# The in-chunk products A on all four quarters of TensorE's array, in two banks, with ScalarE carrying half of them across partitions

## The reference

```python
def step(S, inp):
    r_t, w_t, k_t, v_t, a_t, b_t = inp
    Sa = jnp.einsum("bhvk,bhk->bhv", S, a_t)
    S = S * w_t[:, :, None, :] + Sa[..., None] * b_t[:, :, None, :] + v_t[..., None] * k_t[:, :, None, :]
    y = jnp.einsum("bhvk,bhk->bhv", S, r_t)
    return S, y
...
h = rms_norm(x, g_mix[i])
proj = h @ w_in[i]
y_a = rwkv7_time_mix(proj[..., :RW_COLS], ...)
y_b = dilated_mixture_attention(proj[..., RW_COLS:], slopes)
gate_a, gate_b = jnp.split(jax.nn.sigmoid(h @ w_gate[i] + b_gate[i]), 2, axis=-1)
merged = gate_a * (y_a @ w_branch_a[i]) + gate_b * (y_b @ w_branch_b[i])
x = x + merged @ w_out[i]
x = x + conv_glu_ffn(rms_norm(x, g_ffn[i]), w_up[i], conv_w[i], conv_b[i], w_down[i])
ple_gate = jax.nn.sigmoid(rms_norm(x, g_ple[i]) @ w_ple_gate[i])
x = x + ple_gate * (p[i] @ w_ple[i])
```

## Time and profile before

| what | value |
|---|---|
| median of three runs | 955.06 us |
| profiled execution | 956.54 us |
| its span (first to last instruction) | 954.7 us |
| TensorE busy | 933.7 us, 98% of the span |
| VectorE, ScalarE, GpSimd busy | 43%, 45%, 40% |
| mean granted TensorE clock | 0.997 |

### The profile page before, as it was taken

One profiled execution on the slowest core, in us unless ns is written; L12 is line 12 of the kernel. 1 busy time (PEld: TensorE's weight loads), 2 busy tenths in 40 slices (PEclk: granted clock), 3 DMA queues, 4 the chain that ended last, 5 costly groups with the idle time before them and its releaser, 6 DMA issues.

```text
span 954.7 us, 15908 instructions
## 1 busy us (share of the span) xinstructions
PE 933.7 (98%) x6783; PEld 769.9 (81%) x6783; DVE 409.4 (43%) x645; ACT 428.6 (45%) x683; POOL 384.9 (40%) x180
## 2 busy tenths in 40 slices
PE   6999999999999999999999999999999999999996
PEld 5887888897778778788788888888888888888885
DVE  4223798308565548559244434434344300100435
ACT  6355553235554644623445344443444411412647
POOL 2453444442223526246423444444444444445350
PEclk9999999999999999999999999999999999999998
DMA  7432433332121000226412333333333332323132
GB/s 250 129 92 64 110 88 90 88 90 67 45 59 33 27 25 25 68 71 216 134 44 67 89 106 93 92 107 89 103 96 90 110 110 99 100 89 119 63 105 89
DMA packets 115163, 86.59 MB, mean 91 GB/s; under 512 B 2852, under 2 KB 100022, under 8 KB 115094
## 3 DMA queue, kind: packets, MB, share of 16 engines
q1 hardware_dynamic: 114904, 85.50, 30.3%
q10 hardware_dynamic: 190, 0.08, 0.0%
HBM read 83.47 MB, written 2.10 MB: 90 GB/s over the span
## 4 chain that ended last, share of the span: by engine, by line
PE 95%; ACT 2%; DVE 1%; POOL 1%; DMA 1%; issue 0%; SPq 0%; DVEq 0%
PE bank L544 19%; PE bank L545 18%; PE bank L546 18%; PE bank L606 9%; PE bank L607 9%; PE bank L608 9%; PE bank L863 2%; PE bank L734 1%; PE bank L771 1%; PE bank L819 1%; PE bank L748 1%; POOL w_lo L524 1%; DMA xs<-in_x_dram 1%; PE bank L860 1%; PE bank L904 0%; PE bank L830 0%
## 5 line engine op out<-in xcount | busy, mean ns | idle before, releaser
L524 POOL TENSOR_TENSOR w_lo<-raw,w_hi 128x1024 fp32r<-128x1024 f32 x137 | 330.5, 2412 | 490.4 <-ACT w_hi L1144 490.3
L1144 ACT ACTIVATE w_hi<-raw 128x1024 fp32r<-128x1024 f32 x137 | 145.4, 1061 | 339.6 <-issue 201.2
L544 PE MATMUL bank<-hT_hi,w_hi 128*128 128x512 f32 (+1 forms) x720 | 282.1, 392 | 1.2 <-POOL w_lo L524 1.0
L546 PE MATMUL bank<-hT_hi,w_lo 128*128 128x512 f32 (+1 forms) x720 | 277.0, 385 | 0.0
L545 PE MATMUL bank<-hT_lo,w_hi 128*128 128x512 f32 (+1 forms) x720 | 277.0, 385 | 0.0
L544 PEld LDWEIGHTS bank<-hT_hi,w_hi 128*128 128x128 f32 x720 | 135.2, 188 | 29.3 <-issue 1.7
L546 PEld LDWEIGHTS bank<-hT_hi,w_lo 128*128 128x128 f32 x720 | 135.3, 188 | 27.1
L545 PEld LDWEIGHTS bank<-hT_lo,w_hi 128*128 128x128 f32 x720 | 135.4, 188 | 25.1
L2052 DVE SCALAR_TENSOR_TENSOR cbuf<-bank,params,cbuf 128x511 f32<-128x511 f32 x48 | 36.0, 750 | 132.9 <-ACT cbuf L1542 132.9
L606 PE MATMUL bank<-w_hi,g_hi 128*128 128x512 f32 x184 | 71.7, 390 | 0.0
L608 PE MATMUL bank<-w_hi,g_lo 128*128 128x512 f32 x184 | 71.6, 389 | 0.0
(11 more groups left out here) (318 smaller groups left out, 1350.4 us busy)
## 6 DMA issues: line engine op xcount, KB each, us to landing
raw<-in_w_up_dram SPq DMA_DIRECT2D x48, 512.0 KB, 3.8
raw<-in_w_in_dram SPq DMA_DIRECT2D x33, 512.0 KB, 4.0
raw<-in_w_down_dram SPq DMA_DIRECT2D x24, 512.0 KB, 3.8
raw<-in_w_gate_dram SPq DMA_DIRECT2D x16, 512.0 KB, 4.0
raw<-in_w_out_dram SPq DMA_DIRECT2D x8, 512.0 KB, 4.1
raw<-in_w_ple_gate_dram SPq DMA_DIRECT2D x8, 512.0 KB, 4.2
xs<-in_x_dram SPq DMA_DIRECT2D x4, 512.0 KB, 5.3
raw<-in_w_branch_a_dram SPq DMA_DIRECT2D x4, 512.0 KB, 3.4
```

Of the source, the lines that this page charges most:

```text
L524: nc.gpsimd.tensor_tensor(low(n)[:, :], raw[:, n % RAW_SLOTS, :], high(n)[:, :].bitcast(F32), ALU.subtract).then_inc(*step("pool", ("lo", n)))
L544: nc.tensor.matmul(o, wh, ah, start=first, stop=False)
L546: return nc.tensor.matmul(o, wl, ah, start=False, stop=last)
L1144: nc.scalar.activation(high(u)[:, :], raw[:, u % RAW_SLOTS, :], ACT.Copy) \
```

## The change

`product_a` now takes two banks per group. The products of one chunk are no longer kept to the two quarters on the diagonal: a product of head q (rows of half q) and chunk s is written to the columns of half s. The bank is the first where s = q and the second where s is not q. ScalarE reads them with three copies: the first bank with all 128 partitions, and the two halves of the second bank each into the other half of the partitions, so that `Am` again holds head q in half q. In `Am`, `XT` and `Xs` chunk s of head q now lies in slot s xor q of its group, so `solved_u` picks `Xs` by `c % 2 ^ q`.

```diff
-                o = begin("A", g)
-                head_products(o, lambda s, p, q: KK[half(q), p, chunk_cols(2 * g + s)],
-                              lambda s, p, q: Kb[half(q), p, 2 * g + s, 0, :]).then_inc(*step("pe", ("A", g)))
+                o = [begin("A", g, slot) for slot in range(2)]
+                for p in range(NPAIR):
+                    for s, q in ((0, 0), (1, 1), (1, 0), (0, 1)):
+                        mm = nc.tensor.matmul(o[s ^ q][half(s), p * CH:(p + 1) * CH], KK[half(q), p, chunk_cols(2 * g + s)],
+                                              Kb[half(q), p, 2 * g + s, 0, :], start=True, stop=True)
+                mm.then_inc(*step("pe", ("A", g)))
...
-                        mm = nc.tensor.matmul(o[q][half(0), p * CH:(p + 1) * CH], Xs[half(q), c // 2, c % 2, p, :],
+                        mm = nc.tensor.matmul(o[q][half(0), p * CH:(p + 1) * CH], Xs[half(q), c // 2, c % 2 ^ q, p, :],
...
-                nc.scalar.activation(flat(Am[:, g, :, :, :]), psum(("A", g))[:, :], ACT.Copy) \
-                    .then_inc(*frees("act", ("A", g), ("Am", g)))
+                nc.scalar.activation(Am[:, g, 0, :, :].rearrange("p h t -> p (h t)"), psum(("A", g, 0))[:, 0:256], ACT.Copy) \
+                    .then_inc(*frees("act", ("A", g, 0)))
+                nc.scalar.activation(Am[half(0), g, 1, :, :].rearrange("p h t -> p (h t)"), psum(("A", g, 1))[half(1), 0:256],
+                                     ACT.Copy).then_inc(*step("act"))
+                nc.scalar.activation(Am[half(1), g, 1, :, :].rearrange("p h t -> p (h t)"), psum(("A", g, 1))[half(0), 0:256],
+                                     ACT.Copy).then_inc(*frees("act", ("A", g, 1), ("Am", g)))
```

More of the change, by code:

```diff
@@ L786, in _ @@
             token_units([("v1", s) for s in range(2)], [("vt1", m) for m in range(NT)], hT_hi, hT_lo, 4, 256)
[L792 to L800, removed]
             def chunk_cols(c):
```

## The result

| | before | after |
|---|---|---|
| median | 954.79 us (22 runs, 953.18 to 955.8) | 963.25 us (22 runs, 952.96 to 967.68) |
| profiled execution | 956.54 us | 963.06 us |
| its span | 954.7 us | 961.2 us |
| mean granted TensorE clock | 0.997 | 0.987 |

A forecast was written before the change was run, and what follows sets the result against it. TensorE, busy 98% of the span, was taken as the bound. Products -1.9 us, waiting for `Xs` +1.9, later start +0.1 gave +0.1 us: median 955.2 us, range 953.2 to 957.0.

The forecast's parts named there:

- TensorE's products, 0.49 us a group: Products A on TensorE: four groups take 1.96 us, 0.49 each instead of 0.93, so 1.9 us less work.
- ScalarE's copies, 1.215 us a group: Copies to `Am` on ScalarE: three per group, 1.215 us from group to group, 4.86 us in all instead of 2.4.
- `Am` as late as the identity: Group 0: `Am` ready 0.15 us later than before, arriving together with GpSimd's identity, so VectorE's masked copy starts no earlier.
- the possible 0.25 us: Partial gain possible if VectorE's masked copy takes 0.80 us, as in its last run, and not 1.05.
- The gain turns into waiting: TensorE rests 0.6 us before A's fourth group and 1.3 us before `level_w(0, 0)`, cancelling 1.9 us saved; start 0.1 later.
- No other cost: Later `Am` groups, first `Wp`, bank reuse, recurrence start and `solved_u`: all covered or unaffected, adding nothing.
- The lateness it caused at the last `Am`: Copies to `Am`: the last ready at 297.41 instead of 296.42, 1.0 us if waited for; left out as covered.
- The clock's rival: TensorE's two rests before `level_w(0, 0)` bring its clock to half speed, losing some 2.7 us: 957.9 us; chance 6%.
- The prediction's own sign of this: Prediction is wrong if PEclk shows under 1.00 near 295 us; TensorE's busy time should drop about 1.9 us.
- The price of 2.7 us: Loss if the clock falls: a stretch of 5.6 us at about half speed, as in the kernel's opening with 128x512 products.

The follow-up runs named there:

- pairs: Changed kernel with matmuls reordered so that only the two quarters on one diagonal work at a time, same banks and copies; 954.14 us, ratio 1.0003.
- one_fill: Changed kernel with one gate part (three 128x512 matmuls) moved from the recurrence into TensorE's second rest, ahead of level_w(0, 0); 953.94 us, ratio 0.9986.
- before_rest: Kernel before, with VectorE's transpose of group 0 repeated three more times so TensorE waits once, 2.12 us; 968.39 us, ratio 1.0137.
- rest_dense: before_rest with 24 extra 128x512 matmuls, results thrown away, behind level_w(0, 0); 966.17 us, ratio to the kernel before 1.011.
- gate_fill: Changed kernel with two gate parts (three 128x512 matmuls each) moved from the recurrence into TensorE's two rests; 953.25 us, ratio 0.999.
- ffn_rest: The two kernels ffn_rest_2 and ffn_rest_4: kernel before with a TensorE rest put into the feed-forward part; 960.74 and 963.25 us.
- rest_15: Kernel before, with VectorE's transpose of group 0 repeated two more times, one TensorE rest of 1.38 us; 964.6 us, ratio 1.0086.
- ffn_rest_2: Kernel before, with TensorE waiting for five extra VectorE operations between dense feed-forward products, a 4.4 us rest; 960.74 us, ratio 1.0067.
- old_moved: Kernel before, products A unchanged, with the two gate parts moved ahead of A(3) and level_w(0, 0) as in gate_fill; 954.96 us, ratio 0.9991.
- repeat_fill: Changed kernel with the third group of A computed twice and the fourth three times, to fill the rests; 955.78 us, ratio 1.0039.
- ffn_rest_4: Kernel before, with TensorE waiting for nine extra VectorE operations between dense feed-forward products, a 6.2 us rest; 963.25 us, ratio 1.0096.

## Why the prediction was wrong

- **TensorE's products, 0.49 us a group: right.** 96 rows take 1.63 us, 0.54 a group with the end of the last one in it; A(3) takes 0.69 in the same measure.
- **ScalarE's copies, 1.215 us a group: right.** The copies of one group and the next start 1.21 us apart (12 copies from 291.11 to 295.94, 4.83 us), and the last `Am` is ready at 295.94, 5.59 us behind the first A; the prediction had 297.41 - 291.82 = 5.59.
- **`Am` as late as the identity: right.** `Am` came 1.95 us behind the first A, as worked out, and VectorE was released by it. The masked copy took 1.03 us, not 0.80, so the possible 0.25 us were not gained. In `pairs` the same copy took 0.79.
- **The gain turns into waiting: right, a little large.** 0.47 and 1.02 us of rest where 0.6 and 1.3 were forecast, and `level_w(0, 0)` at 3.81 us against 3.83, forecast at 3.93. The forecast counted a rest from where the next row would have started, the trace counts it from the end of the last row, some 0.2 us later. The six runs whose clock stayed up confirm the sum: their middle, 954.53, is that of before.
- **No other cost: right.** The page "TensorEngine Tiling (Array Packing)" of the Trainium skill, section "PSUM Bottleneck", says that packing doesn't speed up the emptying of the banks. The trace agrees, with ScalarE's copies back to back for 4.8 us. The lateness it caused at the last `Am` was covered, as the prediction said: in `one_fill`, whose clock stayed up, TensorE shows no wait for the copies behind it. The one it caused at the first is the rest of TensorE.
- **The clock's rival: mechanism right, chance and price wrong. This is the step that failed.** The sum put the loss by a fall of the clock at nothing, and the rival that has it was given 6%, because a rest of 1.0 us at 391.5 had left the clock at 1.00. That row has one rest of 1.0 between dense products; here it was 1.49 in all, between 64x64 products. The runs give 73% (16 of 22). Its other row, the fall 2.6 us after the last matmul, was taken as the length of a rest that acts; 1.38 us were enough in 7 of 11 runs. The prediction's own sign of this came: PEclk under 1.00 near 295 us, and TensorE's busy time 5.9 us up where 1.9 less was forecast.
- **The price of 2.7 us** was taken from the opening, where dense 128x512 products come back to speed after 5.6 us. (The page's PEclk has a 9 in its first slice, which holds those matmuls, so the half speed of the opening is read from their starts alone.) Here 64x64 products and gate parts follow, and the clock was low for 20.5 us in the profiled execution. The six slowest runs have no trace; their mean clock, 0.982 where 0.9975 is usual, gives an estimate of (0.9975 - 0.982) x 966 / 0.5 = 30 us, near the 30.7 of `before_rest`. That cost 8.7 us (middle of the group 963.2, less 954.5) in the ten runs and 12.4 (966.9 - 954.5) in the six slowest: 0.4 us for each us at half clock in both. The mis-sized term is thus the length, 20.5 us and not 5.6. In `rest_dense`, with dense work behind the rest, it was 3.4 us: the opening's row was of that kind, and priced another kernel than this one.

What stays open: whether the 64x64 products ahead of the rest make the fall likelier than dense ones would (no kernel had a rest of 1 to 2 us between dense products, beside the one of the earlier trace rows), whether the second rest alone would do it, and why the same kernel falls in some runs and not in others.

## What to carry to other kernels

- On an engine that is busy 98% of the time, saved work that turns into waiting isn't free: ask what fills the hole. Two rests of 0.5 and 1.0 us between small products cost 9 to 12 us in 16 of 22 runs; with independent matmuls moved into them nothing was lost (0 of 22 runs fell in `gate_fill` and `one_fill`).
- Price a fall of the clock by rows with the same kind of work behind the rest. The row from a dense stretch gave 2.7 us where the stretch of 64x64 products lost 8.7 or 12.4.
- Look at each run's mean clock before explaining a median: here the median stood for only one of three groups, and the other two lay 9 us below it and 4 us above, and the chain of waits looked the same in both kernels.

## What the runs showed of the hardware that was not expected

- The time at half clock came in few lengths: 3.4 us (`rest_dense`), 6.8 (both of `ffn_rest`), 20.5 (after) and 30.7 (`before_rest`). The mean clocks of the slower runs of after lie in two groups that roughly fit the last two, and so do those of `before_rest` and `rest_15`.
- In the changed kernel the clock fell about 1 us after the second rest had ended, in the middle of busy work; in `before_rest` within 0.2 us of its end. In `ffn_rest_2`, with 4.4 us, it fell within the rest.
- In `pairs`, with two quarters at work at a time, 96 rows took 2.15 us, where `old_moved`, also with two quarters but with one bank a group, took 3.02 (and the packed form 1.63). The expectation had them equal. Why isn't shown.
- A fresh rest of 0.98 us appeared in `repeat_fill` amid its 112 products, with no semaphore behind it.
- A VectorE operation on two SBUF operands took 2.45 us instead of 0.42 when it started just behind GpSimd's 2.36 us work on a weight block (`ffn_rest_2`, and the same in `ffn_rest_4`), and both ended within 0.3 us of each other.
